# Low parts of the odd LayerNorm tiles made by GpSimd, two tiles behind its additions

## The reference, cut to what matters

```python
x = layer_norm(ALPHA * x + 0.5 * swiglu(x, w_in[l, 0], w_out[l, 0]), g[l, 0], b[l, 0])
y = mixer(x)                       # mLSTM in layer 0, window attention in layer 1
x = layer_norm(ALPHA * x + y, g[l, 1], b[l, 1])
x = layer_norm(ALPHA * x + 0.5 * swiglu(x, w_in[l, 1], w_out[l, 1]), g[l, 2], b[l, 2])
```

## Time and profile before

| | us |
|---|---|
| median of 3 runs (3673.79 to 3674.9) | 3674.51 |
| the profiled execution | 3675.54 |
| its span, first to last instruction | 3673.7 |
| PE busy | 3481.3 |
| DVE busy | 1885.7 |
| ACT busy | 1305.1 |
| POOL busy | 91.2 |

### The profile page before, as it was taken

The page is one execution under the profiler, slowest core; times in us unless marked ns, Lnnn a source line. Parts: engine busy times, 40 slices in busy tenths (PEclk is TensorE's granted clock), DMA queues, the critical chain, the costliest instruction groups (busy, mean ns, idle before and its releaser), DMA issues.

```text
span 3673.7 us, 43393 instructions
## 1 busy us (share of the span) xinstructions
PE 3481.3 (95%) x17554; PEld 2845.8 (77%) x17554; DVE 1885.7 (51%) x3014; ACT 1305.1 (36%) x2205; POOL 91.2 (2%) x128
## 2 busy tenths in 40 slices
PE   8988888999987899999999998999999999999998
PEld 6656668888865688888888866888888888778887
DVE  6664676443676354335433535644364436564446
ACT  4442433222443342224222443422242225543333
POOL 0000000000100000000000100100010001010000
PEclk9999999999988999999999999999999999999999
DMA  3102112233310122332333211233323232013244
GB/s 121 52 29 74 54 45 82 96 98 103 107 54 1 40 92 98 98 104 98 95 100 98 88 53 39 81 98 98 103 86 98 98 103 83 30 53 109 98 138 161
DMA packets 92891, 308.19 MB, mean 84 GB/s; under 512 B 16142, under 2 KB 17940, under 8 KB 92692
## 3 DMA queue, kind: packets, MB, share of 16 engines
q1 hardware_dynamic: 89528, 301.77, 25.0%
q10 hardware_dynamic: 3164, 3.64, 0.3%
HBM read 303.14 MB, written 2.10 MB: 83 GB/s over the span
## 4 chain that ended last, share of the span: by engine, by line
PE 79%; DVE 13%; ACT 4%; issue 2%; DMA 0%; ACTq 0%; DVEq 0%; POOL 0%
PE ps L304 22%; PE ps L305 22%; PE ps L306 22%; PE ps L301 13%; DVE XT L763 1%; DVE WL L292 1%; ACT WH L286 1%; DVE mb_cv L1639 1%; PE ps L2556 1%; DVE XL L769 1%; DVE R L629 0%; DVE XL L771 0%; ACT od_p L2159 0%; DVE S L638 0%; DVE od_t L2351 0%
## 5 line engine op out<-in xcount | busy, mean ns | idle before, releaser
L304 PE MATMUL ps<-XH,WH 128*128 128x512 f32 (+1 forms) x3200 | 1191.7, 372 | 41.8 <-DVE XL L769 25.8
L305 PE MATMUL ps<-XL,WH 128*128 128x512 f32 (+1 forms) x3200 | 1176.8, 368 | 0.0
L306 PE MATMUL ps<-XH,WL 128*128 128x512 f32 (+1 forms) x3200 | 1176.1, 368 | 0.0
L292 DVE TENSOR_TENSOR WL<-RAW,WH 128x1024 fp32r<-128x1024 f32 x568 | 689.1, 1228 | 336.4 <-ACT WH L286 333.2
L304 PEld LDWEIGHTS ps<-XH,WH 128*128 128x128 f32 x3200 | 611.0, 191 | 151.9 <-DVE XL L769 19.1
L306 PEld LDWEIGHTS ps<-XH,WL 128*128 128x128 f32 x3200 | 611.1, 191 | 98.4
L305 PEld LDWEIGHTS ps<-XL,WH 128*128 128x128 f32 x3200 | 611.4, 191 | 96.5 <-issue 1.7
L286 ACT ACTIVATE WH<-RAW 128x1024 fp32r<-128x1024 f32 x568 | 587.2, 1049 | 144.2 <-DMA RAW<-units 62.4
L304 PE MATMUL ps<-HH,WH 128*128 128x512 f32 (+1 forms) x990 | 362.7, 366 | 0.0
L305 PE MATMUL ps<-HL,WH 128*128 128x512 f32 (+1 forms) x990 | 361.8, 365 | 0.0
L306 PE MATMUL ps<-HH,WL 128*128 128x512 f32 (+1 forms) x990 | 361.7, 365 | 0.0
(11 more groups left out here) (579 smaller groups left out, 3515.2 us busy)
## 6 DMA issues: line engine op xcount, KB each, us to landing
RAW<-units SPq DMA_DIRECT2D x568, 512.0 KB, 3.3
XIN<-in_x ACTq DMA_DIRECT2D x2, 1024.0 KB, 6.3
out<-YT SPq DMA_DIRECT2D x8, 256.0 KB, 3.2
GB<-in_ln_g SPq DMA_DIRECT2D x1, 512.0 KB
GB<-in_ln_b SPq DMA_DIRECT2D x1, 512.0 KB
da_pi<-in_positions ACTq DMA_DIRECT2D x1, 256.0 KB, 3.1
mb_pairf<-constants ACTq DMA_DIRECT2D x1, 256.0 KB
wa_dist<-constants ACTq DMA_DIRECT2D x1, 192.0 KB, 2.3
```

Of the source, the lines that this page charges most:

```text
L292: nc.vector.tensor_tensor(WL[:, u % RING, :], RAW[:, u % RING, :], WH[:, u % RING, :].bitcast(F32), ALU.subtract)\
L304: nc.tensor.matmul(out, wh, xh, start=start, stop=False)
L305: nc.tensor.matmul(out, wh, xl, start=False, stop=False)
L306: return nc.tensor.matmul(out, wl, xh, start=False, stop=stop)
```

## The change

In the five LayerNorms, XL of the odd tiles is now made by POOL, in a list `POOL_ORDER` that says in what order POOL does its 16 additions and 8 subtractions; DVE keeps XL of the even tiles. POOL's order is add 0, 1, 2, 3, low 1, add 4, 5, low 3, add 6, 7, low 5, add 8, 9, low 7, add 10, 11, low 9, add 12, 13, low 11, add 14, 15, low 13, low 15. All of POOL's steps count in t_ready; PE and ACT wait there by position in that list. Before it overwrites an XT buffer DVE now waits explicitly for the XH that reads it.

```diff
+        def x_wait(pe, e, t):
+
+            if e["ln"] and t % 2:
+                pe.wait_ge(S["t_ready"], e["at0"] + POOL_ORDER.index(("low", t)) + 1)
+            else:
+                pe.wait_ge(S["x_ready"], e["x0"] + (t // 2 if e["ln"] else t) + 1)
...
@@ first_units
-                pe.wait_ge(S["x_ready"], x0 + k + 1)
+                x_wait(pe, nrm, k)
...
-                pe.wait_ge(S["x_ready"], x0 + KD + k + 1)
+                x_wait(pe, nrm, KD + k)
...
@@ gpsimd
-                    for t in range(16):
-                        x = XT[:, t % 4, :]
-                        pool.wait_ge(S["ln_scaled"], 16 * lns + t + 1)
-                        nc.gpsimd.tensor_tensor(x, x, NB[:, t // 8, :], ALU.add).then_inc(S["t_ready"], 1)
+                    for what, t in POOL_ORDER:
+                        x, k, hs = XT[:, t % 4, :], t % 8, HALVES[t // 8]
+                        if what == "add":
+                            pool.wait_ge(S["ln_scaled"], 16 * lns + t + 1)
+                            nc.gpsimd.tensor_tensor(x, x, NB[:, t // 8, :], ALU.add).then_inc(S["t_ready"], 1)
+                        else:
+                            pool.wait_ge(S["xh_ready"], 16 * e["c"] + t + 1)
+                            nc.gpsimd.tensor_tensor(XL[:, k, hs], R[:, k, hs], XH[:, k, hs].bitcast(F32), ALU.subtract)\
+                                .then_inc(S["t_ready"], 1)
...
@@ scalar, norm
-                    act.wait_ge(S["t_ready"], 16 * e["c"] + t + 1)
+                    act.wait_ge(S["t_ready"], e["at0"] + (POOL_ORDER.index(("add", t)) if e["ln"] else t) + 1)
...
@@ vector, norm
                     if t + ahead < (8 if t < 8 else 16):
+                        if ln and t:
+                            dve.wait_ge(S["xh_ready"], 16 * e["c"] + t)
                         normed(t + ahead)
-                    if not final:
+                    if not final and not (ln and t % 2):
                         low(t)
...
                     if t == 7:
                         chain(e, 1)
+                        if ln:
+                            dve.wait_ge(S["xh_ready"], 16 * e["c"] + 7)
                         for i in range(8, 8 + ahead):
                             normed(i)
...
+POOL_ORDER = [s for t in range(16) for s in ([("add", t)] + ([("low", t - 2)] if t % 2 and t > 2 else []))] + [("low", 15)]
```

More of the change, by code:

```diff
@@ L242, in build @@
         TAIL = dict(load=8, ffn=1, ev_attn=0, ev_mamba=3, od=3, win=3, mlstm=3)
+        x_count = at_count = 0
         r_count = sq_count = add_count = tail_count = norm_count = f_count = nr_count = 0
@@ L269, in build @@
                 e["c"], e["prod"], e["nr0"] = norm_count, prod, nr_count
+                e["x0"], e["at0"] = x_count, at_count
+                x_count += KD if e["ln"] else 16
+                at_count += len(POOL_ORDER) if e["ln"] else 16
                 prod["norm"] = e
@@ L330, in first_units @@
             nrm = e["behind"]
-            x0 = 16 * nrm["c"]
             def half(u, k, hs):
```

## The result

The changed kernel takes 3698.46 us (median of 6 runs, 3697.4 to 3702.3); the kernel before took 3674.32 (6 runs) beside it. The ratio is 1.0067, interval 1.0055 to 1.0079: **24.1 us slower**. The profiled execution took 3698.14 us, its span is 3696.3.

A forecast was written before the change was run, and what follows sets the result against it. PE was taken to bound the kernel, busy 3481.3 of 3673.7 us. Stall 12.3 plus clock 7.7 made 20.0 us on the profiled 3675.54, 3695.5; that execution lay 1.0 above the median, so 3694.5 us, range 3684 to 3704.

The forecast's parts named there:

- 12.3 us of stall: PE's net added idle over the five LayerNorms: 3.0 + 3.0 + 2.7 + 1.8 + 1.8 us.
- The queue order: XL of tile 7 queues behind additions 8 and 9, which wait for the second chain; PE idles 5.0 us, net 3.0.
- POOL's subtraction: POOL's new XL operations cost what its additions do: 0.97 us, or 0.87 us apart when they follow each other.
- ln01 and ln11: LayerNorms behind a mixer: tile 3 comes earlier from POOL, the second chain starts 1.2 us earlier, leaving 1.8 us each.
- ln10: LayerNorm without low clock in the first half: chain can start up to 0.5 us earlier, so 2.7 us instead of 3.0.
- The clock: One low-clock stretch of 3.4 us behind each new PE idle, 1.5 us each (bounds 0 and 2.2), 7.7 in all.
- The port: DVE and POOL blocking each other on their shared port: taken as 0, upper bound 0.8 us each LayerNorm (4 us).
- DVE would be busy 17 us less: Profile sign: DVE loses 40 subtractions of 0.43 us, so its busy time falls by about 17 us.
- The port rival: DVE and POOL block each other before tile 7, POOL's subtraction is slower, clock at upper bound: 3703 us, chance 0.12.
- Faster: Rival: DVE, relieved, starts the second chain up to 3.6 us earlier (deciding point 3.1); 9.4 us won, 3665; chance 0.03.

The follow-up runs named there:

- e1: Changed kernel with XL of tile 7 moved ahead of the addition of tile 8 in POOL's list; 3676.91 us, ratio 1.0006.
- e2: Changed kernel with XL of tile 7 given back to DVE, the other seven odd tiles staying on POOL; 3678.72 us, ratio 1.0011.
- e4: Changed kernel with XL of tile 7 one place earlier in POOL's list, behind the addition of tile 8; 3694.44 us.
- e5: Changed kernel with XL of tile 7 one place later in POOL's list, behind the addition of tile 10; 3702.05 us.
- e3: Changed kernel with 40 matmuls whose result nobody reads put in front of PE's wait for tile 7; 3686.72 us.
- e8: e1 with unread matmuls in PE's waits: 18 or 12 before tile 0, 15 before tile 4 behind a mixer; 3672.11 us, ratio 0.9993.
- e6: Changed kernel with POOL making XL of tiles 1, 3 and 5 only, DVE the rest; 3673.75 us, ratio 0.9998.
- e9: e6 with unread matmuls in PE's waits: 18 or 12 before tile 0, 15 before tile 4 behind a mixer; 3672.88 us, ratio 0.9992.

## Why the prediction was right

Forecast 3694.5 us (3684 to 3704), measured 3698.46.

The terms were 12.3 us of stall and 7.7 us of clock, 20.0 in all; measured were about 13 and 11. Both were too small, and nothing cancelled. (The 7.7 is 1.5 each for five, which is 7.5; the forecast carries the slip of 0.2.)

- *The queue order.* Right, and shown by e1, e2, e4 and e5. Counted from PE's start on tile 0 the chain of ln00 begins at 9.03 us (8.94 before; I had it unchanged). XL of tile 7 ends 6.93 us behind the start of the chain (forecast 6.95), the idle is 4.95 us (5.0), and the waits for tiles 8 and 11 are gone.
- *POOL's subtraction.* Taken from the nearest row, the addition: 0.87 us apart in both cases. Its group has 40 in 39.7 us, mean 996 ns, forecast 0.97; the pairs that meet DVE's weight split are longer.
- *ln01 and ln11.* The step that failed, though it is small. I gave them 1.2 us for a second chain that starts earlier. Its start behind PE's tile 0 is 12.24 us (2339.79 less 2327.55) where it was 12.45 before: 0.2 us. Tile 3 came early and the wait was 2.15 us for 2.2 forecast, but the clock was low through all of tile 4 and the first half of PE's sums (2335.0 to 2338.4; the sums run from 2337.16 to 2339.67), where before it was low only to the start of the sums. ln10 gave 0.1 us instead of 0.3. So the plain stall is 12.3 + 2.0 + 0.2 = 14.5 us by these steps; e3 leaves 13.2 us over before in the table.

```profile
2339.79 0.42 DVE L760 TENSOR_SCALAR VA<-ps 128x256 f32<-128x256 f32 x1 [1.98 <-PE ps L312]
```

- *The clock.* The mechanism was right and its size too small: 1.5 us each, where e3 takes away 11.1 to 12.6 in all. This is the term with the largest miss. The stretches behind the stall held 4.2 to 5.3 us of PE's work, half of which is 2.1 to 2.7 us each, 12.2 in all; my bound was 2.2. I had taken the length of 3.4 us from the kernel before, where the idle was 2.4 to 2.8. Here the clock was low for 6.8 us in each of the five places, and only 1.5 us (ln00) to 2.5 us (ln10) of that lay inside the idle:

```profile
2041.50:2048.30 6.80, 5.31 (x25) 5.31 (x26) 6.41 (x7) 5.98 (x12) 6.80 (x8) 0.50 0.00 1
3096.20:3103.00 6.80, 4.26 (x20) 4.26 (x21) 6.37 (x8) 5.48 (x10) 6.80 (x8) 0.50 0.00 0
```

- *The port.* I took 0, and for the changed kernel that was right: from tile 8 on, PE waits for no tile. But the forecast that DVE would be busy 17 us less was wrong: 7.3 us. DVE's remaining XL take 669 ns in the mean, from 499, and those 56 are 9.5 us longer together:

```profile
L784 DVE TENSOR_TENSOR XL<-R,XH 128x256 fp32r<-128x256 f32 x56 | 37.4, 669 | 5.5 <-ACT XH L611 3.3
L515 POOL TENSOR_TENSOR XL<-R,XH 128x256 fp32r<-128x256 f32 x40 | 39.7, 996 | 0.0
```

  I also read the earlier trace rows wrongly. XL started at 2033.51, 0.05 us ahead of the addition, so its 0.42 us says nothing against a hold of the whole instruction. What the rows point to as held is the addition, with 0.96 us: XL of tile 5 in the changed kernel, beside which DVE was idle until its last 0.05 us, took 0.74:

```profile
2032.68 0.74 POOL L515 TENSOR_TENSOR XL<-R,XH 128x256 fp32r<-128x256 f32 x1
```

  So the 0.90 to 0.99 us that I took for POOL's operation already had DVE's share in it. The forecast of 0.87 us apart held since DVE's work beside it is the same.

  The port rival had 3703 for the changed kernel; e1 shows that its price, 3.8 us in the table, is paid once the stall is gone, in the second half where the weight splits lie.
- *Faster.* Refuted for this chain: DVE had 1.07 us to spare at the second chain of ln00 and waited for PE's sums. Even at full clock (e8) the chain moved up by 0.47 us, where 3.1 would have been needed.

What stays open: how the medians of e1, e2, e6 and e9 are ordered, since they were timed on different chips and differ by less than their runs do; the two groups of e3's runs; and where the clock falls in the first half, which differs from execution to execution (ln10 has no low stretch in the kernel before and one in the changed kernel, with the same wait of 2.38 us ahead of it).

## What to carry to other kernels

When work is moved to an idle engine, write down its list beside the consumer's and ask of each entry what the entries ahead of it wait for: a lag of "two tiles" that is harmless inside a stage becomes a wait for the next stage's start at its edge. The idle share of the receiving engine says nothing on that. And a stall of the bounding engine is to be priced with the slow clock behind it, which here nearly doubled it, while a low stretch in front of a wait that another engine sets costs nothing.

## What the runs showed of the hardware

- Behind 4.95 us of idle PE worked at 1.2 GHz for 4.2 to 5.3 us in all five places; behind 4.08 us (e4) it was 3.2 to 6.0 us, behind 5.82 us (e5) 3.1 to 5.1 us, so a longer idle wasn't followed by more low clock. Behind 2.38 to 2.79 us in the kernel before it was 3.4 us or none. A short idle was once followed by as much: in ln11 of e3 PE waited 2.14 us and then worked at 1.2 GHz for 6.1 us (3304.90 to 3311.00, granted 0.50). Matmuls that nobody reads, put into the wait, kept the clock at 1.00 behind it.
- A DVE operation and a POOL operation, both with two inputs in SBUF, hold each other up, and the one that starts second is the one held. A DVE subtraction of 1024 columns takes 1.23 us alone and 1.65 us when it starts 0.42 us into a POOL addition (before), and 1.64 when it starts 0.36 us into one (e1). A POOL subtraction of 256 columns takes 0.74 us when DVE is idle beside it, about 0.9 us between DVE's operations of 256 columns, and 1.71 us when it starts 0.52 us into the DVE subtraction of 1024. In the prediction only DVE was taken to be held up.
